# Seven block products for the delta rule's q, k, v and z on tokens padded to 770

## The reference, cut to what matters

```python
p = u @ w_in                                   # 512 latent + 256 context tokens, 1024 features
qkv = silu(centred_dwconv(p[..., :4096], conv_w))   # five taps along the tokens
z = p[..., 4096:6144]
q, k = l2_norm(q), l2_norm(k)                  # 8 heads of 128, each serving two v heads
t_inv = triangular_solve(eye + a, eye)         # per chunk of 64 tokens, per head, two directions
...                                            # a scan over the chunks gives o
y = (rms_norm(o, o_norm_g) * silu(z)) @ w_out
```

## Time and profile before

| | |
|---|---|
| median of 3 runs | 2926.69 us (2923.0 to 2927.52) |
| profiled execution, its own time | 2928.49 us |
| its span | 2926.7 us |
| PE matmul busy | 2800.1 us, 96% |
| DVE, ACT, POOL busy | 1446.7, 978.7, 249.6 us |
| mean granted TensorE clock | 0.989 of full speed |

### The profile page before, as it was taken

How to read it: one execution, slowest core, us unless ns; L and a number is a source line. 1 busy time by engine, 2 the same in 40 slices (tenths; PEclk the granted TensorE clock), 3 DMA queues, 4 the chain that set the end, 5 groups by cost and what they waited for, 6 DMA issues and landing times.

```text
span 2926.7 us, 39634 instructions
## 1 busy us (share of the span) xinstructions
PE 2800.1 (96%) x16306; PEld 1972.7 (67%) x16306; DVE 1446.7 (49%) x2980; ACT 978.7 (33%) x2531; POOL 249.6 (9%) x172
## 2 busy tenths in 40 slices
PE   8899999999999999999999989999999999999998
PEld 3677778787777867664645335578677664688886
DVE  3466574756657464633334244533357321677732
ACT  1436455463636544003234123322223311211200
POOL 0000000000000000000000022113112220000031
PEclk9999999999999999999999999999999999999999
DMA  5101111110111232502100001112132111221220
GB/s 224 46 10 49 61 22 45 23 45 22 50 29 49 79 109 98 201 29 93 58 29 22 31 23 72 58 58 86 73 115 87 43 72 58 95 89 61 99 103 29
DMA packets 76341, 193.74 MB, mean 66 GB/s; under 512 B 56096, under 2 KB 60960, under 8 KB 64512
## 3 DMA queue, kind: packets, MB, share of 16 engines
q1 hardware_dynamic: 52720, 181.92, 17.0%
q10 hardware_dynamic: 23440, 9.28, 1.2%
HBM read 181.22 MB, written 9.96 MB: 65 GB/s over the span
## 4 chain that ended last, share of the span: by engine, by line
PE 89%; ACT 6%; DVE 4%; issue 1%; DMA 1%; SPq 0%; DVEq 0%; ACTq 0%
PE ps L1722 9%; PE ps L1922 9%; PE ps L1190 8%; PE ps L1247 7%; PE ps L1285 6%; PE ps L1469 5%; PE ps L1950 4%; PE ps L1248 4%; PE ps L1739 3%; PE ps L1862 3%; ACT arena L1979 2%; PE ps L1600 2%; PE ps L1328 2%; PE ps L1338 2%; PE ps L1299 2%; PE ps L1350 2%
## 5 line engine op out<-in xcount | busy, mean ns | idle before, releaser
L1979 ACT ACTIVATE arena<-ps 64x64 f32<-64x64 f32 (+7 forms) x1011 | 327.0, 352 | 766.8 <-PE ps L1722 164.1
L1722 PE MATMUL ps<-arena 128*128 128x256 f32 x1456 | 327.6, 379 | 2.0 <-ACT arena L1979 2.0
L1722 PEld LDWEIGHTS ps<-arena 128*128 128x128 f32 x1456 | 270.6, 190 | 40.1 <-issue 5.7
L1247 PE MATMUL ps<-arena 128*128 128x512 f32 x512 | 263.8, 597 | 1.7 <-DVE arena L2629 1.7
L1922 PE MATMUL ps<-arena 128*128 128x256 f32 x1176 | 254.5, 378 | 0.0
L1922 PEld LDWEIGHTS ps<-arena 128*128 128x128 f32 x1176 | 222.2, 189 | 32.6 <-issue 0.5
L1190 PE MATMUL ps<-arena 128*128 128x512 f32 x496 | 222.4, 608 | 14.7 <-DVE arena L2985 5.1
L1190 PEld LDWEIGHTS ps<-arena 128*128 128x128 f32 x496 | 95.9, 194 | 139.6 <-issue 130.3
L1980 ACT ACTIVATE arena<-ps,arena 128x128 f32<-128x128 f32 x544 | 156.6, 381 | 86.1 <-PE ps L1403 45.7
L1248 PEld LDWEIGHTS ps<-arena 128*128 128x128 f32 x512 | 97.2, 190 | 124.5 <-issue 124.5
L1285 PE MATMUL ps<-arena 128*128 128x256 f32 x768 | 178.0, 385 | 0.0
(11 more groups left out here) (351 smaller groups left out, 4294.2 us busy)
## 6 DMA issues: line engine op xcount, KB each, us to landing
arena<-in_ada_w SPq DMA_DIRECT2D x12, 2048.0 KB, 9.6
arena<-in_w_up SPq DMA_DIRECT2D x11, 2048.0 KB, 8.1
arena<-in_w_dil SPq DMA_DIRECT2D x9, 2048.0 KB, 8.0
arena<-in_w_dn SPq DMA_DIRECT2D x8, 2048.0 KB, 10.2
arena<-in_w_gate SPq DMA_DIRECT2D x6, 2048.0 KB, 8.0
arena<-in_w_down SPq DMA_DIRECT2D x4, 2816.0 KB, 9.6
arena<-in_att_in SPq DMA_DIRECT2D x5, 2048.0 KB, 8.1
arena<-in_w_z SPq DMA_DIRECT2D x8, 1024.0 KB, 4.9
```

Of the source, the lines that this page charges most:

```text
L1247: e.matmul(ps[:, b1, :], w, uT[:, k * T_ALL + 256:(k + 1) * T_ALL], start=k == 0, stop=k == 7)
L1722: m = e.matmul(ps[:, bank, 0:256], left[:, k], right[:, k], start=first and k == 0, stop=k == 3, skip_group_check=not first)
L1979: return e.activation(out, x, ACT.Copy)
```

## The change

q, k, v of stages 1 to 7 and z of all stages are computed by seven block products instead of eight. The 1024 features are split in two halves, the tokens in two halves, and two tiles of 128 output features form a pair. The tokens are padded to 770 (two zero columns between context and latent tokens), so that a half is 385 columns. A pair costs seven products `P1` to `P7` of 4 matmuls of 385 columns each (`pair_product`); POOL forms the sums of weights (`sums`, four additions of 512 columns for each pair) and, once, the sums of inputs `T1` to `T4` (1540 columns); the results are gathered by four ACT copies (`pair_snap`) and four DVE additions (`pair_add`) of 385 columns. `P6`, `P7` and `P4` accumulate onto `P1` in one bank, each after the copy of what stands there. Stage j has three pairs: (k, 0) is q and k, (k, 1) the two v tiles, (j, 2) is z.

z is now laid out features by tokens, so the gate and the gain are applied after the transposes (`fin_y` on DVE) and not before them; ACT's copy of y, POOL's product and one of DVE's two multiplications in `gate_o` are gone. The products of q, k and v stand in the solve, those of z in the joins; `silu` and `turn` of v have moved from the joins of the stage before to the solve.

```diff
+SEVEN = ("P1", "P2", "P6", "P5", "P7", "P3", "P4")
...
         yield "clean", j
-        yield "blocks", j
-        if j == 0:
-            yield "silu", 0, 2, 3
-        if j:
-            yield "sum_sq", j - 1
-        yield from p[1 if 0 < j < 7 else 0:4]
...
         if j:
             yield "zg", j - 1
-        early = {3: 4, 5: 5, 8: 6, 10: 7, 12: 8, 14: 9}
...
+        if j < 7:
+            yield "silu", j, 2, 3
+            yield from unit(k, 0, "P2") + unit(k, 0, "P6")
+            if j:
+                yield "sum_sq", j - 1
+            yield "pair_add", k, 0, "P2"
+            yield from unit(k, 0, "P5")
+            yield "pair_add", k, 0, "P5"
+            if j:
+                yield "gate_o", j - 1
+            yield from unit(k, 0, "P7")
+            yield "pair_add", k, 0, "P7"
+            yield "blocks", j
+            yield from unit(k, 0, "P3")
+            yield "solve", j, 1
+            yield "pair_add", k, 0, "P3"
+            yield from unit(k, 0, "P4")
+            if j:
+                yield "finish", j - 1
+            for i in range(2, 9):
+                yield "solve", j, i
+            yield from unit(k, 1, "P1") + unit(k, 1, "P2") + unit(k, 1, "P6")
+            for i in range(9, 16):
+                yield "solve", j, i
+            yield from unit(k, 1, "P5")
+            yield "solved", j
+            yield "pair_add", k, 1, "P2"
+            if j:
+                yield "fin_y", j - 1
+            yield "turn", j, 0
+            yield "turn", j, 1
+            yield "pair_add", k, 1, "P5"
+            yield from conv(k, 0)
+            yield from unit(k, 1, "P7")
+            yield "pair_add", k, 1, "P7"
+            yield from unit(k, 1, "P3")
+            yield "pair_add", k, 1, "P3"
+            yield from unit(k, 1, "P4")
+
+            t = [x for n in range(1, 4) for x in conv(k, n)]
+            behind = [zh[:2] + t[:4], zh[2:4] + t[4:5], z_add("P2") + [("silu", k, 0, 1)] + zh[4:7] + t[5:9],
+                      z_add("P5") + zh[7:10] + z_add("P7") + t[9:11], zh[10:12] + t[11:12],
+                      z_add("P3") + zh[12:] + t[12:] + [("norm_sq", k, 0)],
+                      [("norm", k, 0), ("norm_x", k, 0), ("norm_sq", k, 1)], [("norm", k, 1), ("norm_x", k, 1)], []]
+            if k == 7:
+                behind[8] = [("silu", 7, 2, 3), ("turn", 7, 0), ("turn", 7, 1)]
...
+            for i in range(1, 16):
+                yield "solve", 7, i
+                yield p[3 + i]
+                if i == 2:
+                    yield "finish", 6
...
+            def pair_product(j, p, name, part):
+
+                (a, b, c), (a_, b_) = pair_banks(j, p), pair_weights(j, p)
+                s = [quarter(S_dn, n) for n in range(4)]
+                bank, left, right, n, first, event = {
+                    "P1": (a, a_[:, 0], U_H[:, 0, :, 0], None, True, "snap1"),
+                    "P2": (c, a_[:, 1], U_H[:, 1, :, 0], None, True, "c11"),
+                    "P6": (a, s[1], T2, 1, False, "snap2"),
+                    "P5": (b, s[0], T1, 0, True, "c22"),
+                    "P7": (a, s[2], T3, 2, False, "snap3"),
+                    "P3": (c, s[3], U_H[:, 1, :, 1], 3, True, "c12"),
+                    "P4": (a, b_[:, 1], T4, None, False, "c21")}[name]
...
+                    take_banks(bank)
+                for k in range(2 * part, 2 * part + 2):
+                    m = e.matmul(ps[:, bank, 0:HALF_PAD], left[:, k], right[:, k], start=first and k == 0, stop=k == 3,
+                                 skip_group_check=not first)
...
+            def pair_snap(j, p, name):
...
+                if p == 0:
+                    for n in range(2, 4):
+                        e.wait_ge(*at("conv", j - 1, n))
...
+                copy(pair_half(j, p, place_), ps[:, pair_banks(j, p)[0], 0:HALF_PAD]).then_inc(*mark(f"pair_{event}", j, p))
...
+            def fin_y(j):
...
+                e.scalar_tensor_tensor(o1, t[:, :, 256:768], V("o_norm"), g[:, :, 258:770], MUL, MUL)
```

More of the change, by code:

```diff
@@ L23 @@
     "mod": "mod sc mu0",
-    "dn": "proj raw pads tap conv silu nrm turn v kn z S0 osum osq ored orstd onrm gated fin y",
+    "dn": "proj raw pads tap conv silu nrm turn v kn z pair osum osq ored orstd onrm fin y",
     "inv": "inv solve solved spread clean unit0 unit",
@@ L267, in conv, with unit @@
         return [("conv", j, n, q) for q in range(first, last)]
[L269 to L273, removed]
+    def unit(j, p, name):
+        return [("pair", j, p, name, part) for part in range(2)]
     def norms(j, n):
@@ L314, in dn_order @@
+    yield from (("exp", 0, 3), *scaled(0, 2), ("gram", 0, 3), *scaled(0, 3), *grams(5), ("exp", 0, 5))
+    yield from (("gram", 0, 5), *scaled(0, 5), *unit(1, 0, "P1"), *conv(0, 3))
     for j in range(8):
         k = j + 1
[L317 to L320, removed]
-            if j:
[L322 to L336, removed]
@@ L349, in dn_order @@
[L349 to L358, removed]
-            if i == 6 and j == 0:
-                yield "turn", 0, 0
-                yield "turn", 0, 1
-            if i == 8 and j:
-                yield "gate_o", j - 1
-            if i == 12 and j == 7:
-                yield "mod_turn", 4
-                yield "mod_turn", 5
-            if i == 14 and j:
-                yield "finish", j - 1
@@ L574, in program @@
         mark_raw = top[0]
-        raw = [take(774), take(774)]
-        cv = [take(770) for _ in range(4)]
+        conv_buf = [take(774) for _ in range(6)]
         at_sqA = top[0]
@@ L747, in program @@
             SLOT_OF["dn_out", n] = 1 - n % 2
+        for name, slot in (("dn", 1), ("z", 0)):
+            for j in range(8):
+                SLOT_OF[name, j] = slot
+        SLOT_OF["ada", 5] = 1
         SLOT_OF["w_ukv", 0] = 0
@@ L1490, in tensor_program @@
                     kn(*which)
-                elif what == "z":
-                    z(*which)
+                elif what == "pair":
+                    pair_product(*which)
                 elif what == "decay":
@@ L2239, in scalar_program @@
                     kn(*which)
-                elif what == "z":
-                    j, c, part, b = which
-                    if c % 2 and part == 3:
-                        z(j, c, b)
+                elif what == "pair":
+                    if which[3]:
+                        pair_snap(*which[:3])
                 elif what == "zg":
@@ L2280, in scalar_program @@
                     sum_sq(*which)
-                elif what == "finish":
-                    finish(*which)
             for n in range(8):
@@ L2795, in scan_o @@
                 e.wait_ge(*at("scan_o_pe", j, s))
+                if s == 0 and 0 < j < 7:
+                    e.wait_ge(*at("y_out", j - 1))
                 for d in range(2):
@@ L2862, in vector_program @@
                     gate_o(*which)
+                elif what == "fin_y":
+                    fin_y(*which)
+                elif what == "pair_add":
+                    pair_add(*which)
             def slab_sums(n):
@@ L3321, in pool_program @@
             e.wait_ge(*at("mu0_u", 7))
-            for r in raw:
+            for r in conv_buf:
                 e.memset(r[:, 0:2], 0.0)
```

324 lines of the change are left out of this document (203 added, 121 removed).

## The result

The changed kernel took 2993.27 us (median of 4 runs, 2987.02 to 2997.15), the kernel before 2927.11 beside it (2923.0 to 2929.78): 1.0225 of the time before, 95% interval 1.0204 to 1.0247, that is 66 us slower. I had forecast 2952, with 2906 to 2984 as the range. The sign came, the size did not.

A forecast was written before the change was run, and what follows sets the result against it. PE sets the pace. Stages 1 to 6 add 2.6 us each (15.6), stage 6's end 6.7, stage 0 1, stage 7 2: +25 us on 2928.5, 2954; less 1.8 for the median, 2952 us. Range 2906 to 2984.

The forecast's parts named there:

- The products: q, k, v and z matmuls: 0.325 us a record, 2.60 a product, 61 us of PE work saved in all.
- The rival of 385 columns at the price of 512: Block products: 154 products cost 0.86 us more each, 132 us, giving 3084 us; chance 0.05.
- The waits of a stage: PE in stages 1 to 6: 7.6 us at P7, 1.1 at second transposes of v, 2.4 at second norm, among others.
- join x: Joins of a middle stage: P4 covers ACT's copies that the size-64 join x waited for, 1.1 us less.
- ACT is in time: Solve, stages 1 to 6: P6's copy ready when P5 ends, the 7.6 us waits fall away, 2906 us; chance 0.15.
- the errors cancel: Middle stages: with two terms 2 us too large, a stage ends near no change, 2927 us; chance 0.16.
- Sum: 43.6 - 2 x 2.55 + 1.5 + 7.6 + 1.1 = 48.7 us: Solve of stages 1 to 6: products saved, transposes and two waits added, 48.7 us for 43.6 before.
- the sum of the joins behind it: Joins of stages 1 to 6: 51.0 - 3.2 - 1.5 - 1.1 + 2.4 + 0.9 = 48.5 us.
- +1, between -3 and +4: Stage 0: first join at 182.7 for 185.97, then 18.2 us of z in place of 14.3; +1 us.
- POOL holds DVE: Four of twelve POOL additions a stage hold what PE waits for: 32 us, giving 2984 us; chance 0.13.
- +6.7: End of stage 6: silu and transposes of v for stage 7 behind the last join, nothing beside them; +6.7 us.
- +2: Stage 7 and tail: first join at 1089.1 for 1086.14, less 1 for a product gone from the tail; +2 us.

The follow-up runs named there:

- late_loads: Changed kernel, in stages 1 to 6 silu of v moved behind P3 of the first pair and zg behind P1 of the second: 2934.98 us, 1.0026 of before.
- all_and_turn: all_queues plus half of P7 of the second pair put between the two groups of six transposes of v: 2902.6 us, 0.9902 of before.
- small_sums: Changed kernel, POOL forms one column of each sum of weights from the second pair on (wrong results): 2987.86 us, 1.0191 of before.
- filled_wait: Changed kernel, 11 unread matmuls of 385 columns on PE before P7 of the first pair, stages 1 to 6: 2986.63 us, 1.0192 of before.
- set_inputs: Changed kernel, in stage 0 POOL writes zeros into T1, T2 and T4 instead of forming sums of inputs: 2990.72 us, 1.0206 of before.
- all_queues: Changed kernel with late_loads, early_squares and, in stage 7, zg moved behind the solve's step 6: 2910.22 us, 0.993 of before.
- early_squares: Changed kernel, DVE forms the squares of k before it multiplies q by its norm: 2967.0 us, 1.0129 of before.

## Why the prediction was right or wrong

**The products: right.** 2.60 us a product of 8 records were forecast, 0.324 a record were measured where PE did not wait (late_loads). In a whole stage PE's work fell from 127.61 to 119.63 us (all_and_turn), 7.98, where I had 2 x 2.55 + 3.2 = 8.3. The rival of 385 columns at the price of 512 is out.

**The waits of a stage: right.** My walk had 10.9 us more idle time in a stage. The windows have 137.00 - 122.61 = 14.39 us of idle time for 130.18 - 127.61 = 2.57: 11.8 more. `P7`, the norm and the scan came within 0.12 us. Two terms were off by half a us: the second transposes, 1.65 for 1.1, which small_sums puts down to POOL's sums (1.05 without them), and join x, whose 1.1 us less I had taken for idle time; of it only 0.5 was (0.24 and 0.25 in the trace before), and the rest stands in PE's busy time. That also settles "ACT is in time" and "the errors cancel": neither happened.

**The step that failed: "Sum: 43.6 - 2 x 2.55 + 1.5 + 7.6 + 1.1 = 48.7 us" and the sum of the joins behind it price every instruction at the full clock.** They add 10.9 us to an idle time of 2.57 us a stage and leave the speed of the work behind it as it was; none of the five rivals has the clock either. The kernel before runs its stages 1 to 6 at 1.00, and PE never stands still in them for longer than 1.22 us. The term that is missing is 2.98 us a stage by the windows of stage 4; a stage was forecast to grow by 2.6 and grew by 6.8 (stage 4), 7.2 in the mean. Shown by filled_wait (same wait, same neighbours, PE busy: full clock) and by late_loads (58 us gained for 46 of waiting). Stages 1 to 6 missed (7.2 - 2.6) x 6 = 27 us of the 43 between the forecast +25 and the measured +69, and the low clock, 2.98 x 6 = 18, is two thirds of that; the waits that came out longer (11.8 for 10.9) and the products that saved less (7.98 for 8.3) make another 7. The other misses are stage 0 with 8, the end of stage 6 with 4, and stage 7 with the tail, 4.

The trace of before had the warning ready. In its stage 0, the same 16 records of a Gram step, behind a wait and in a scan:

```profile
109.04 3.51 PE L1299 MATMUL ps<-arena 128*128 128x128 f32 x16 [2.06 <-ACT arena L1980]
...
238.92 1.95 PE L1299 MATMUL ps<-arena 128*128 128x128 f32 x16
```

1.56 us more behind one wait was there to be read. It was in my own rows too: 96 records of the first join take 3.01 us in the earlier trace rows and 4.29 behind a wait of 3.33 in the earlier trace rows. How often such a wait costs clock one trace doesn't tell: in the traces of set_inputs and all_queues the same 16 records, behind the same 2.06 us, run at 1.00 and take 2.33. Of the clock the Trainium skill (Trainium Architecture — The Big Picture, section What this means for kernel authors) says: "PE runs at 1.2 or 2.4 GHz depending on recent activity"; filled_wait agrees (1.00 with PE at work in the wait, 0.83 in the kernel after). The sentence gives no price of a wait.

**Stage 0, "+1, between -3 and +4": wrong, +8.8.** I took DVE's taps of v as they end in the kernel before, 148.0, and did not carry what POOL now does from 125.7 on: three sums of 1540 columns and four of 512. The mechanism was in my text, as the rival "POOL holds DVE", but only for the sums of weights, not for the sums of inputs in stage 0. set_inputs shows 4 to 6 us of it in the trace. The clock was low as well (0.66 of full between 131.15 and 152.09, 0.91 in the kernel before from 129.66 to 148.10), and set_inputs did not change that (0.63 up to `P6`). And my sum had left out the second norm's wait, which stands in stage 0 as in the others (2.28 us at 232.80): of the 7.8 us missed, 6.3 lie before the first join and 1.8 behind it (49.84 us to the scan for 44.10 + 3.9), but for rounding.

**Stage 6, "+6.7": undersized.** It is 17.8 - 7.2 = 10.6 us over an ordinary stage. The silu and transposes are where I put them (wait 5.68); new is the second norm's wait of 4.42 for 2.28, POOL's by small_sums (DVE's product 2.04 us for 0.96), and low clock from there to the scan.

**Stage 7 and the tail, "+2": undersized, +6.1.** `finish` waits 7.55 us as written (7.6), but the transposes and the modulation behind it run at the low clock (2.82 us for the forecast 1.4 at `finish` alone), and PE waits 2.36 for the copy before `P6`, for which I had 1.5.

**POOL holds DVE (2984 as a whole): partly right.** small_sums gives it 5 to 10 us and set_inputs up to 6, not 32.

What stays open: when the clock falls behind a wait, and for how long. With the same waits the five middle stages of the kernel after last 136.2 to 139.3 us in one execution, and the same 2.03 us at the scan cost clock in three stages of all_queues and not in the other three. No run tells what decides it.

## What to carry to other kernels

Price a forecast wait of a PE that has had none at more than its length, and look in the same trace for work behind a wait to see how much more; here 7.64 us of waiting cost 10.0, and 2.28 cost 3.6 in the mean of five stages. Where blocks accumulate on one bank through copies, the copies become part of PE's critical chain: nothing that can stand elsewhere (table loads, gates, norms) may stand before them in the copying engine's order. Then the trade paid after all: two moved entries a stage turned 2.25% slower into 0.26% slower, and the squares and the transposes with them (and a gate in stage 7) into 1.0% faster, with the same arithmetic.

## What the hardware showed that I had not expected

- Behind a wait of 3.28 us the 24 records took 9.54 us, behind one of 7.64 us 9.25 to 10.74. Halving the wait did not halve the clock's cost.
- A wait of 2.02 us at the scan's start, without the one of 2.28 us some 5 us earlier, left the clock at full in five scans of six in early_squares and in three of six in all_queues. With both, it was low (0.79) in the first 8 us of all six scans of small_sums.
- Eleven useless matmuls in the wait gave the next 24 records their 7.87 us back.
- A DVE product of 512 columns with two SBUF inputs lasted 3.81 us beside a POOL sum of 1540 columns that takes 3.77, and 0.69 where POOL wrote zeros instead.
